# Router transpositions moved inside the next tile's output products, with sixteen products of a zero matrix around the last tile's

## What is computed

```python
mix = (g_ssm * y_ssm + g_att * y_att) @ w_o[l]
h = layer_norm(DEEPNORM_ALPHA * h + mix, ln1_g[l], ln1_b[l])
ffn = moe_ffn(h, w_router[l], b_router[l], w_up[l], b_up[l], w_down[l], b_down[l])
h = layer_norm(DEEPNORM_ALPHA * h + ffn, ln2_g[l], ln2_b[l])
```

## Time and profile before

| | |
|---|---|
| median of 3 runs | 1724.87 us (1720.63 to 1724.88) |
| profiled execution, its own time | 1721.2 us |
| its span, first to last instruction | 1719.4 us |
| TensorE, VectorE, ScalarE, GpSimd busy | 96%, 88%, 63%, 30% |
| mean granted TensorE clock | 0.983 of full |
| the stretch of the change in this span | 451 to 528 us |
| the expert loop | 566 us to about 1692 us |

### The profile page before, as it was taken

How to read it: one execution, slowest core, us unless ns; L and a number is a source line. 1 busy time by engine, 2 the same in 40 slices (tenths; PEclk the granted TensorE clock), 3 DMA queues, 4 the chain that set the end, 5 groups by cost and what they waited for, 6 DMA issues and landing times.

```text
span 1719.4 us, 22463 instructions
## 1 busy us (share of the span) xinstructions
PE 1650.9 (96%) x7233; PEld 1106.9 (64%) x7233; DVE 1508.3 (88%) x1683; ACT 1077.1 (63%) x1036; POOL 507.6 (30%) x321
## 2 busy tenths in 40 slices
PE   5899899999999899999999999999999999999996
PEld 2334347766676677777777777777777777777763
DVE  5999889765778899999999999999999999999995
ACT  5323234376455677777777777777777777777771
POOL 4855134482524022132221212212131121211210
PEclk9999899999999999999999999999999999999998
DMA  5111112312137899999999999999999999999973
GB/s 176 49 52 49 50 50 99 121 52 103 41 128 277 347 373 355 359 388 364 368 365 369 378 360 370 361 366 376 355 369 361 373 379 357 367 366 376 375 280 107
DMA packets 91902, 464.78 MB, mean 270 GB/s; under 512 B 21289, under 2 KB 21405, under 8 KB 42616
## 3 DMA queue, kind: packets, MB, share of 16 engines
q1 hardware_dynamic: 80240, 441.67, 67.3%
q0 software_dynamic: 9776, 18.41, 4.4%
q10 hardware_dynamic: 1848, 4.24, 0.7%
HBM read 454.15 MB, written 18.53 MB: 275 GB/s over the span
## 4 chain that ended last, share of the span: by engine, by line
PE 85%; DVE 10%; issue 2%; ACT 1%; DMA 1%; POOL 0%; ACTq 0%; DVEq 0%; POOLq 0%
PE ps L1848 20%; PE ps L1850 20%; PE ps L1849 20%; PE ps L1834 3%; PE ps L1548 2%; PE ps L1856 2%; PE ps L1529 2%; PE ps L1543 2%; PE ps L1631 1%; PE ps L1633 1%; PE ps L1632 1%; DVE w_lo L1255 1%; PE ps L1623 1%; PE ps L1537 1%; PE ps L1750 1%
## 5 line engine op out<-in xcount | busy, mean ns | idle before, releaser
L1255 DVE TENSOR_TENSOR w_lo<-raw,w_hi 128x2048 fp32r<-128x2048 f32 x384 | 873.6, 2287 | 73.7 <-ACT w_hi L898 72.6
L898 ACT ACTIVATE w_hi<-raw 128x2048 fp32r<-128x2048 f32 x384 | 737.0, 1919 | 240.1 <-PE ps L1850 239.7
L1848 PE MATMUL ps<-w_hi,x_hi 128*96 128x512 f32 x1024 | 414.0, 404 | 1.2 <-DVE w_lo L1255 1.2
L1850 PE MATMUL ps<-w_lo,x_hi 128*96 128x512 f32 x1024 | 403.0, 394 | 0.0
L1849 PE MATMUL ps<-w_hi,x_lo 128*96 128x512 f32 x1024 | 402.4, 393 | 0.0
L637 POOL DMA_INDIRECT gate_now<-gate_rows,row_now x32 | 79.7, 2490 | 454.6 <-DVE tok_out L1396 439.4
L1848 PEld LDWEIGHTS ps<-w_hi,x_hi 128*96 128x96 f32 x1024 | 168.1, 164 | 69.0 <-DVE w_lo L1255 2.4
L1850 PEld LDWEIGHTS ps<-w_lo,x_hi 128*96 128x96 f32 x1024 | 165.4, 162 | 70.8 <-issue 0.2
L1848 PE MATMUL ps<-w_hi,a_hi 128*96 128x512 f32 x512 | 204.4, 399 | 5.7 <-DVE a_lo L1366 5.7
L1849 PEld LDWEIGHTS ps<-w_hi,x_lo 128*96 128x96 f32 x1024 | 165.8, 162 | 63.6
L1849 PE MATMUL ps<-w_hi,a_lo 128*96 128x512 f32 x512 | 201.6, 394 | 0.0
(11 more groups left out here) (337 smaller groups left out, 2208.0 us busy)
## 6 DMA issues: line engine op xcount, KB each, us to landing
raw<-in_w_up SPq DMA_DIRECT2D x256, 1024.0 KB, 8.1
raw<-in_w_down SPq DMA_DIRECT2D x128, 1024.0 KB, 9.6
ring<-in_w_in SPq DMA_DIRECT2D x9, 2048.0 KB, 7.8
ring<-in_w_glu SPq DMA_DIRECT2D x4, 1024.0 KB, 6.3
ring<-in_w_o SPq DMA_DIRECT2D x2, 2048.0 KB, 12.3
h<-in_x SPq DMA_DIRECT2D x4, 512.0 KB, 5.5
ring<-in_w_attn_proj SPq DMA_DIRECT2D x1, 2048.0 KB, 7.9
h_rows<-h ACTq DMA_DIRECT2D x4, 512.0 KB, 2.7
```

Source lines behind the costliest of these rows:

```text
L898: s.activation(hi_of(c)[:, :], raw_of(c), ACT.Copy).then_inc(s_hi, 1)
L1255: d.tensor_tensor(lo_of(c)[:, :], raw_of(c), hi_of(c)[:, :], ALU.subtract).then_inc(s_lo, 1)
L1848: mm(o, xh, hi_of(c)[:, col], start=start, stop=False)
L1850: return mm(o, xh, lo_of(c)[:, col], start=False, stop=stop)
```

## The change

Three edits on TensorE's list, none on another engine's. `route_T(t - 1)` is called inside `w_out(t)`, in the second half ahead of step k = 4, so 36 products of the tile stand ahead of it and 12 behind, and no longer after `w_out(t)`. `no_rows(n)` makes n products of 128x384 of the zero matrix `none_b`, added to bank 2: ten ahead of `route_T(3)` and six behind it.

```diff
@@ w_out(t), in the loops over r and k
                         if t == 0:
                             pe.wait_ge(s_wolo, KD * r + k + 1)
+                        if t > 0 and r == 1 and k == KD // 2:
+                            route_T(t - 1)
                         x, o = slice(P * t, P * t + P), ps[2 + i % 4]
@@ behind w_out
+            def no_rows(n):
+
+                for _ in range(n):
+                    mm(ps[2][:, 0:4 * BLK], ones_b[:, :], none_b[:, :], start=False, stop=False)
@@ the loop over the tiles
                 if t > 0:
-                    route_T(t - 1)
                     route_lg(t - 1)
@@ after the loop
             first_rows(0)
+            no_rows(10)
             route_T(TT - 1)
+            no_rows(6)
             place(TT - 2)
             route_lg(TT - 1)
```

## The result

| | kernel before | changed kernel |
|---|---|---|
| median of 22 runs each, in turns | 1723.94 us (1719.81 to 1727.14) | 1726.58 us (1724.00 to 1730.01) |
| profiled execution, its own time | 1721.2 us | 1724.51 us |
| its span | 1719.4 us | 1721.7 us |
| mean granted TensorE clock | 0.983 | 0.985 |

The ratio is 1.0017, 95% interval 1.0010 to 1.0024: the changed kernel is slower by 0.10 to 0.24%, some 2.9 us (the medians differ by 2.6). That is less than the 0.3% named in the prediction, but its sign is clear.

A forecast was written before the change was run, and what follows sets the result against it. Before the loop, VectorE's and GpSimd's chains end together at 541.5; VectorE's gains 1.7 us, GpSimd's loses 0.9, so +0.9: 1722.1 on the profiled execution, 1725.8 on the median. The forecast took 1724, range 1719 to 1729.

The forecast's parts named there:

- the 0.3% named in the prediction: Whole kernel: the smallest change a measurement can tell from none, about 0.3% or 5.2 us; "same" given chance 0.78.
- I take the middle, 1724: Final number: 1724 us, between 1722.1 on the profiled execution's own time and 1725.8 on the median.
- The sum: Whole kernel: `slots` and the rest come 0.9 us later, GpSimd's chain deciding; chance 0.3, within 1 us.
- slow stretches in `w_out`: Rival: runs of before hold slow stretches, 1.6 us each, hidden by the new waits; near 1722 in all runs, chance 0.2.
- `slots` +0.9: GpSimd's chain: the last scatter is issued 0.9 us later, so `slots` come 0.9 us later.
- Start of the scatters: GpSimd: scatters begin at 516.34 + 2.9 = 519.25, because `norm1(3)` ends 2.9 us later.
- Last issue: GpSimd: last of twelve scatters issued by 537.95, 0.9 us later than 537.08, with three again slowed by VectorE's subtractions.
- Landing and load: Behind GpSimd's last scatter: landing and reading back taken as 4.45 us, unchanged.
- the 1.7 said: VectorE's chain: comes to `slots` 1.7 us earlier, at 539.65, as `place(3)` on TensorE is earlier with the clock kept.
- The zero products cost nothing: TensorE around `route_T(3)`: ten lie in old idle time, six ahead of `place(2)`, which waits for `choose(2)` anyway; no cost.
- rivals two and three: TensorE: clock falls behind last transpositions, +3.0 us, chance 0.15; or already half at zero products, 5.4 us later, chance 0.08.
- Rival one: GpSimd's chain is not last, scatters falling between VectorE's subtractions: -1.7 us, 1719.5 on the profiled execution; chance 0.15.

The follow-up runs named there:

- e5: Kernel before plus the sixteen zero products, with ScalarE's three small transfers started ahead of the first expert's part 11: ratio to before 0.9996 (0.9988 to 1.0005).
- e6: Changed kernel with ScalarE's three small transfers started ahead of the first expert's part 11: ratio to before 1.0018 (1.0009 to 1.0028).
- e1: Changed kernel without its sixteen zero products, transpositions still inside the next tile's output products: ratio to before 1.0029 (1.0017 to 1.0042).
- e2: Kernel before with the sixteen zero products alone, transpositions where they were: ratio to before 1.0008 (0.9997 to 1.0019).
- e4: Changed kernel with tile 1's addresses computed right behind `first_marks(1)` instead of together with tile 2's: ratio to before 1.0023 (1.0014 to 1.0032).
- e8: Changed kernel with only tile 2's transpositions inside `w_out(3)`, those of tiles 0 and 1 as before: ratio to before 1.0013 (1.0000 to 1.0025).
- e3: Changed kernel with transpositions of tiles 0 and 1 ahead of step 7 instead of 4, tile 2's behind `w_out(3)`: ratio to before 1.0006 (0.9993 to 1.0019).
- e7: e3 without the ten zero products, and with ScalarE's small transfers started ahead of part 11: ratio to before 0.9979 (0.9969 to 0.9990).
- e9: e7 without the edit on ScalarE's queue: ratio to before 0.9982 (0.9971 to 0.9993).
- e12: e7 with ScalarE's transfers and VectorE's `sums(2)` at c == 12, and `route_lg(2)` behind `first_rows(0)`: ratio to before 0.9980 (0.9969 to 0.9990).
- e10: e7 without its six zero products: ratio to before 0.9988 (0.9978 to 0.9998).

## Why the prediction was wrong in its number, and where it was right

**The step that failed is the last one, "I take the middle, 1724".** The sum was +0.9, slower; on the shown median it gave 1725.8. I put the number below that, since I held it possible that slow stretches in `w_out`, which the new waits would hide, made the 3.7 us between profiled execution and median. They don't. The slow stretch is in all four traces that have the old order up to `w_out(3)`, once in each and 1.6 us long, so as far as four traces tell it is part of the kernel's usual time, and the profiled execution had it too. The changed kernel did absorb it, as the prediction has it at tile 3, and was slower all the same. Its runs spread nearly as far (6.0 us against 7.3). In the fourteen traces the first output product alone lies 5.6 us apart, ahead of all that the change touches, while the span behind the loop's start varies by 1.6; what makes the 3.7 us is not shown. The number should have been the sum on the median: 1725.8, on the slower side.

**One term of the sum was mis-sized: `slots` +0.9, measured +2.57.** By its parts:

- Start of the scatters, predicted +2.9, measured +3.32. The waits were 2.05, 0.94 and 2.32 (predicted 1.9, 1.0, 2.4), and the last product of `w_out(3)` ended at 506.42 + 0.39 = 506.81 (507.1 predicted); but the first product had begun 0.84 earlier in that trace, so this is 3.31 later than before, not 2.9. Of the difference, 0.23 was there already when tile 0 was normalised (21.61 from the first product, 21.38 before), ahead of all that the change touches. That the times in the span look right (506.42, 537.88) is partly chance.
- Last issue, predicted +0.9 (537.95), measured 537.88, and +1.64 counted from the first product. The scatters met the same three subtractions, as predicted, one for 2.89 us, ending 0.85 behind `lo(-1, 4)`: 522.67 + 2.89 = 525.56 against 522.42 + 2.29 = 524.71. The Trainium skill ("SBUF — State Buffer", SBUF: two separate sides) has whichever of the two starts second fully blocked, where VectorE's operation has two inputs in SBUF and GpSimd's reads from it. The trace agrees for a scatter that starts during a subtraction. It does not for a subtraction that starts during a scatter: before, `lo(-1, 4)` at 524.21 took 2.28 us with a scatter at GpSimd from 524.05 to 525.03, as long as after, where none was (2.29 at 522.42).
- Landing and load were taken as 4.45 us for good; they took 5.39, +0.94. That the landing isn't a constant is shown by e5 and e6: 4.80 to 1.21 and 3.30 to 1.59 us when ScalarE's transfers move. The prediction gave no reason for taking it as one. Why it was 3.30 after and 2.70 before is not settled: in the eight traces with those transfers at their old place it was 1.89 (e1) to 4.80 (e2). ScalarE started its transfers 0.9 us earlier counted from the first product (gates at 75.3, before 76.2), while the last scatter was 1.6 later.

**The rest of the mechanism held.** VectorE reached `slots` early and waited 3.42 us (2.7 predicted); its chain was earlier, though by less than the 1.7 said (`lo(-1, 4)` 0.95 earlier counted from the first product). The zero products cost nothing and the clock was kept up to 521 us, so rivals two and three did not occur in this trace. Both were close. e4's clock fell behind the zero products. And e6, whose list on TensorE is the changed kernel's, lost its clock inside `w_out(3)` behind a wait of 2.26 us, as e1 did behind 2.33: nine products at 0.5 to 0.6 us, the end of `w_out(3)` 0.6 later. It was back at full when e6's zero products ran. Where the sum says "at full clock" it rests on a clock that two of four traces with this wait did not keep. Rival one (GpSimd not last) was false here.

**What the move was worth.** It removes three pauses of 0.74 us and the slow products of `w_out(3)`, and puts waits of 2.05 + 0.94 + 2.32 in their place, ahead of twelve products for which the critical chain waits: the loss is shown at `w_out(3)` by e1 and e8, and its opposite by e3, e7 and e9 to e12, where the transpositions come nearer to the time at which their input is ready. Of the 3.0 us that these gain at `w_out(3)`, 1.4 are idle time and 1.6 the clock; no run parts the two. What the zero products are worth stays open: at most 2.2 us in one pair of traces, nothing that a median shows.

## What to carry to other kernels

Before an instruction is moved into the work of the next tile to fill a pause, compare the time at which its input is ready with the time at which its engine gets there: here it turned 0.74 us of idle time into 2.3, and the same move three steps later, with the last one left outside, gained 0.2% once the zero products ahead of `route_T(3)` were left out. Where two chains end together, an edit that shortens one only turns up as a longer wait; price the other with its landing as well as its issues. When the effect is smaller than the spread of the runs, count from a milestone ahead of the change, and put the number where the sum says, not halfway to a rival.

## What the runs showed of the hardware

- Landing of small scatters depends on what another queue moves beside them: 1.89 to 4.80 us behind the last issue in the eight traces with ScalarE's rows and gates at their old place, 1.18 to 1.62 in the six where these start later (e5, e6, e7, e10 to e12).
- The 8 KB of gates took very different times to land, early or late: at their old place 7.9 us (e4), 8.3 (e1), 10.2 (before), 14.9 (e3, e9) and 15.7 (e2), at the later one 7.2 (e7), 10.0 (e6), 16.1 (e5) and 25.8 to 26.4 (e10 to e12).
- The granted clock fell in one kernel and not in its neighbour without the length of one pause deciding it. The changed kernel kept it after waits of 2.05, 0.94 and 2.32 us and again after 0.65; e1 and e6 lost it after 2.33 and 2.26 at the same place. Behind `place(2)` it was 0.50 without the zero products (e1), and 0.68 with them but 2.05 us of idle time after them (e4).
- Behind the logits of tile 1 it fell in four traces of four (`w_out(3)`, eight products of 0.63 us, some 3 us long) when a pause of 0.74 us stood ahead of these logits, and in none of ten without it. The same pause ahead of the logits of tile 0 was followed by no such product in `w_out(2)`.
